# Grid attention with half-block column order: 256 keys for every query block, one bias transfer a head

## What is computed

```python
def neighbourhood_attn(q, k, v, rpb):
    rows = S // GRID_W                       # 8
    kr = min(NA_ROWS_MAX, rows)              # 8: every row
    row_start = jnp.clip(r - kr // 2, 0, rows - kr)
    col_start = jnp.clip(c - NA_COLS // 2, 0, GRID_W - NA_COLS)
    in_win = (c[None, :] >= col_start[:, None]) & (c[None, :] < col_start[:, None] + NA_COLS)
    bias = rpb.astype(jnp.float32)[:, dr_idx][:, :, :, dc_idx]
    s = jnp.einsum('brchd,brijhd->bhrcij', qg, kband).astype(jnp.float32) * (D ** -0.5)
    s = s + bias[None]
    s = jnp.where(in_win[None, None, None, :, None, :], s, NEG_INF)
    p = jax.nn.softmax(s.reshape(sh[:-2] + (kr * GRID_W,)), axis=-1).reshape(sh)
    o = jnp.einsum('bhrcij,brijhd->brchd', p.astype(v.dtype), vband)
```

## Time and profile before

| what | value |
|---|---|
| median of 3 runs | 2036.09 us (2034.68 to 2036.15) |
| the profiled execution | 2036.51 us, its span 2034.7 us |
| granted TensorE clock | 0.998 of full speed, mean |
| PE busy | 2008.6 us, 99% of the span |
| DVE, ACT, POOL busy | 54%, 43%, 9% |
| DMA | 175.00 MB, mean 86 GB/s |

### The profile page before, as it was taken

One profiled execution on the slowest core, in us unless ns is written; L12 is line 12 of the kernel. 1 busy time (PEld: TensorE's weight loads), 2 busy tenths in 40 slices (PEclk: granted clock), 3 DMA queues, 4 the chain that ended last, 5 costly groups with the idle time before them and its releaser, 6 DMA issues.

```text
span 2034.7 us, 31733 instructions
## 1 busy us (share of the span) xinstructions
PE 2008.6 (99%) x11679; PEld 1760.7 (87%) x11679; DVE 1091.6 (54%) x1898; ACT 868.4 (43%) x1272; POOL 189.5 (9%) x191
## 2 busy tenths in 40 slices
PE   8999999999999999999999999999999999999998
PEld 8989999999888888889988888888889888888887
DVE  4224788656653666567754433444656654434443
ACT  5534555533222544456743322233656543312233
POOL 0004001210110110001001100110014001100100
PEclk9999999999999999999999999999999999999999
DMA  4322111232333233331023332332322133332332
GB/s 137 98 82 83 53 43 51 64 94 86 94 109 106 87 93 98 113 99 52 12 85 94 100 103 83 93 108 86 100 83 66 34 100 93 104 92 86 100 98 79
DMA packets 321921, 175.00 MB, mean 86 GB/s; under 512 B 6560, under 2 KB 319136, under 8 KB 321840
## 3 DMA queue, kind: packets, MB, share of 16 engines
q1 hardware_dynamic: 321840, 173.92, 29.4%
HBM read 171.80 MB, written 2.10 MB: 85 GB/s over the span
## 4 chain that ended last, share of the span: by engine, by line
PE 67%; ACT 1%; DVE 1%; issue 1%; POOL 0%; POOLq 0%; ACTq 0%; DVEq 0%
PE ps L2086 38%; PE ps L2092 19%; PE ps L2680 3%; PE ps L2640 2%; PE ps L2665 2%; PE ps L2617 1%; PE ps L2618 1%; ACT scaled_heads L1224 1%; PE ps L2559 1%; DVE scaled_heads L1896 1%; PE ps L2718 0%; ACT w_hi L797 0%; PE ps L2204 0%; DVE w_lo L1303 0%; PE ps L2464 0%
## 5 line engine op out<-in xcount | busy, mean ns | idle before, releaser
L2086 PE MATMUL ps<-z_hi,w_hi 128*128 128x512 f32 (+2 forms) x2128 | 643.2, 343 | 0.8 <-DVE qf L1416 0.6
L2086 PE MATMUL ps<-z_lo,w_hi 128*128 128x512 f32 (+2 forms) x2128 | 634.4, 338 | 0.0
L1303 DVE TENSOR_TENSOR w_lo<-raw,w_hi 128x1024 fp32r<-128x1024 f32 (+2 forms) x298 | 384.9, 1292 | 434.6 <-ACT w_hi L797 433.3
L797 ACT ACTIVATE w_hi<-raw 128x1024 fp32r<-128x1024 f32 (+2 forms) x298 | 328.3, 1102 | 441.9 <-PE ps L2092 403.8
L2092 PE MATMUL ps<-z_hi,w_lo 128*128 128x512 f32 (+2 forms) x2128 | 446.1, 339 | 0.0
L2086 PEld LDWEIGHTS ps<-z_hi,w_hi 128*128 128x128 f32 x2128 | 366.4, 188 | 51.8 <-issue 4.2
L2086 PEld LDWEIGHTS ps<-z_lo,w_hi 128*128 128x128 f32 x2128 | 365.0, 188 | 44.8
L2092 PEld LDWEIGHTS ps<-z_hi,w_lo 128*128 128x128 f32 x2128 | 345.1, 188 | 45.3
L2086 PE MATMUL ps<-g_hi,w_hi 128*128 128x512 f32 (+1 forms) x539 | 209.4, 390 | 0.5 <-POOL g_lo L725 0.5
L2086 PE MATMUL ps<-g_lo,w_hi 128*128 128x512 f32 (+1 forms) x539 | 208.7, 389 | 0.0
L725 POOL TENSOR_TENSOR g_lo<-gv,g_hi 128x512 f32 x66 | 85.7, 1298 | 1064.5 <-ACT g_hi L1169 1064.5
(11 more groups left out here) (334 smaller groups left out, 2345.3 us busy)
## 6 DMA issues: line engine op xcount, KB each, us to landing
raw<-w_gate_up SPq DMA_DIRECT2D x88, 512.0 KB, 3.7
raw<-w_down SPq DMA_DIRECT2D x48, 704.0 KB, 4.4
raw<-w_in SPq DMA_DIRECT2D x44, 512.0 KB, 3.7
raw<-w_up SPq DMA_DIRECT2D x44, 512.0 KB, 3.7
raw<-w_out SPq DMA_DIRECT2D x24, 512.0 KB, 3.7
raw<-w_in_b SPq DMA_DIRECT2D x14, 512.0 KB, 3.7
raw<-w_in_a SPq DMA_DIRECT2D x12, 512.0 KB, 3.7
raw<-w_branch SPq DMA_DIRECT2D x8, 512.0 KB, 3.7
```

The costliest lines, as they stand in the source:

```text
L797: act.activation(w_hi[s][:, 0:width], raw[s][:, 0:width], ACT.Copy).then_inc(hi_done, 1)
L1303: dve.tensor_tensor(w_lo[s][:, 0:width], raw[s][:, 0:width], w_hi[s][:, 0:width].bitcast(F32), ALU.subtract).then_inc(lo_done, 1)
L2086: pe.matmul(out, w_hi[s][:, w0 + k * P:w0 + (k + 1) * P], rhs[:, lo:lo + width], start=a, stop=False)
```

## The change

Blocks of keys are now 128 tokens made of two half blocks of 8 columns, and all tokens of layer 1 except queries are turned by one half block: the last half block comes first. Key blocks b and b+1 (modulo 4) then hold columns from 8 before the query block to 8 behind it, so every query block has exactly 256 keys; block 3 takes key blocks 3 and 0 by a backward step. Queries, `q_pair`, are turned back by writing them in two pieces. Exponentials, masked sums, copies, transposes and value products of blocks 1 and 2 shrink with the width. The host lays out the biases as [12, 128, 256], so that one DMA brings a head's, and POOL adds the mask in three instructions of 256 columns. The diff, without what only follows from the new argument `l` of `span` and `key_block`, and without the constants' shapes:

```diff
+HB = BC // 2
         def natural(x):
-            return x.rearrange("p (r b c) -> p b r c", r=GRID_R, b=4)
+            return x.rearrange("p (r b c) -> p b r c", r=GRID_R, c=HB)
         def blocked(x):
-            return x.rearrange("p (b r c) -> p b r c", r=GRID_R, b=4)
+            return x.rearrange("p (b r c) -> p b r c", r=GRID_R, c=HB)
+        TURNED = ((slice(0, 7 * HD), slice(HD, SEQ)), (slice(7 * HD, SEQ), slice(0, HD)))
+        def turned_blocks(x):
+            return ((blocked(x)[:, 1:], slice(0, 7)), (blocked(x)[:, 0:1], slice(7, 8)))
-        def span(memory, b):
-            return (0, NMEM) if memory else ((P, 2 * P), (0, 3 * P), (0, 3 * P), (0, 2 * P))[b]
-        def key_block(memory, b, j):
-            return j if memory else max(b - 1, 0) + j
+        def span(memory, b, l):
+            return (0, NMEM) if memory or l else ((P, 2 * P), (0, 3 * P), (0, 3 * P), (0, 2 * P))[b]
+        def key_block(memory, b, j, l):
+            if memory:
+                return j
+            return (b + j) % 4 if l else max(b - 1, 0) + j
             def bias_load(h, r):
                 sp.wait_ge(*atts[1].at("bias", h - 2))
-                for rq in range(GRID_R):
-                    rows = slice(GRID_R - 1 - rq, 2 * GRID_R - 1 - rq)
-                    sp.dma_start(rpb_raw[r][rq * BC:(rq + 1) * BC, :, :],
-                                 t["rpb"][bass.ds(h, 1), :, rows, :].rearrange("o c r x -> (o c) r x"))\
-                      .then_inc(rpb_loaded[r], 16)
+                sp.dma_start(rpb_raw[r][:, :], t["rpb"][bass.ds(h, 1), :, :].rearrange("o q x -> (o q) x"))\
+                  .then_inc(rpb_loaded[r], 16)
-                        pool.wait_ge(rpb_loaded[r], 128 * g + 128)
+                        pool.wait_ge(rpb_loaded[r], 16 * g + 16)
                         pool.wait_ge(*s.at("ls", 4 * h - 8))
...
+                        for v in range(3):
+                            mask = att_con[:, 3 * P + 4 * HB * v:3 * P + 4 * HB * (v + 1)]
                             x = pool.tensor_tensor(
-                                bias[l][r][:, at_:at_ + n * P].rearrange("p (n r c) -> p n r c", n=n, r=GRID_R),
-                                rpb_raw[r][:, :, x0:x0 + n * BC].rearrange("p r (n c) -> p n r c", n=n),
-                                mask.rearrange("p (n o c) -> p n o c", n=n, o=1)
-                                    .to_broadcast([P, n, GRID_R, BC]), ALU.add)
+                                blocked(bias[l][r][:, v * NMEM:(v + 1) * NMEM]), blocked(rpb_raw[r][:, :]),
+                                mask.rearrange("p (n o c) -> p n o c", o=1, c=HB).to_broadcast([P, 4, GRID_R, HB]),
+                                ALU.add)
                         if order:
-                            z, x, square = (ur, vr)[s][:, 0:tokens], natural(x), blocked(square)
+                            z, x = (ur, vr)[s][:, 0:tokens], natural(x)
...
-                            act.activation(blocked(z), x, ACT.Identity, scale=g(m)).then_inc(sems["z"], 1)
+                            for to, blocks in turned_blocks(z):
+                                done = act.activation(to, x[:, blocks], ACT.Identity, scale=g(m))
+                            done.then_inc(sems["z"], 1)
                             act.wait_ge(*sems.at("z", m + 1))
                             act.activation(hi, z, ACT.Copy).then_inc(sems["z_hi"], 1)
+                            for to, blocks in turned_blocks(square):
+                                done = act.activation(to, x[:, blocks], ACT.Square)
+                            done.then_inc(sems["sq"], 1)
# rounded_heads, ACT:
-                    act.activation(hi, tile, ACT.Copy).then_inc(s["q_hi"], 1)
+                    if l and (m < queries or m >= queries + keys):
+                        for to, of in TURNED:
+                            done = act.activation(hi[:, :, to], tile[:, :, of], ACT.Copy)
+                    else:
+                        done = act.activation(hi, tile, ACT.Copy)
+                    done.then_inc(s["q_hi"], 1)
# rest_heads, DVE:
-                    dve.tensor_tensor(lo, tile, hi.bitcast(F32), ALU.subtract).then_inc(s["q_lo"], 1)
+                    if l and (m < first_key or m >= first_key + keys):
+                        for to, of in TURNED:
+                            done = dve.tensor_tensor(lo[:, :, to], tile[:, :, of], hi[:, :, to].bitcast(F32), ALU.subtract)
+                    else:
+                        done = dve.tensor_tensor(lo, tile, hi.bitcast(F32), ALU.subtract)
+                    done.then_inc(s["q_lo"], 1)
# scores, PE:
+                    if l and not memory and b == 3:
+                        bank = chunked(bank, 2)
+                        hi, rest_ = (chunked(x[:, head, :], 4)[:, ::-3] for x in (hi, rest_))
+                    else:
+                        hi, rest_ = (x[:, head, lo:lo + width] for x in (hi, rest_))
# laid_out, host:
-    padded = np.pad(a["rpb_b_2"][0], ((0, 0), (0, 0), (BC, BC + 1)))
-    out["rpb"] = np.stack([padded[:, :, BC - 1 - c:4 * BC - 1 - c] for c in range(BC)], axis=1)
+    q, key = np.arange(P)[:, None], np.arange(NMEM)[None, :]
+    down = key // HB % GRID_R - q // HB % GRID_R + GRID_R - 1
+    across = key // HD * HB - HB + key % HB - (q // HD * HB + q % HB) + BC - 1
+    out["rpb"] = a["rpb_b_2"][0][:, down, np.clip(across, 0, 2 * BC - 2)]
```

More of the change, by code:

```diff
@@ L202, in build @@
         ls_second = [sb([tails[b]], f"ls1_{b}", [P, 3 * P]) for b in range(4)]
[L203 removed]
+        rpb_raw = [sb([w_at[i] + 4 * UNIT], f"rpb_raw{i}", [P, NMEM]) for i in range(2)] + [rpb_last]
         assert at[0] <= scratch
@@ L1244, in exps @@
                     for b in blocks:
-                        lo, width = span(memory, b)
+                        lo, width = span(memory, b, l)
                         act.activation(ls(r, b)[:, lo:lo + width], ls(r, b)[:, lo:lo + width], ACT.Exp,
@@ L1250, in copy @@
                 def copy(h, memory, b):
-                    _, width = span(memory, b)
+                    _, width = span(memory, b, l)
                     act.wait_ge(*s.at("t", 4 * h + (b + 1)))
@@ L2611, in scores @@
                     memory = n_ >= QH
-                    _, width = span(memory, b)
+                    _, width = span(memory, b, l)
                     bank = banks(r + b)[:, 0:width]
-                    lo = key_block(memory, b, 0) * P
+                    lo = key_block(memory, b, 0, l) * P
                     hi, rest_ = (mk_hi, mk_lo) if memory else (k_hi, k_lo)
                     head = n_ - QH if memory else kv
-                    pe.matmul(bank, q_pair[:, n_, b * P:(b + 1) * P], hi[:, head, lo:lo + width], start=True, stop=False)
-                    pe.matmul(bank, q_pair[:, n_, b * P:(b + 1) * P], rest_[:, head, lo:lo + width],
-                              start=False, stop=True).then_inc(s["s"], 1)
+                    if l and not memory and b == 3:
+                        bank = chunked(bank, 2)
+                        hi, rest_ = (chunked(x[:, head, :], 4)[:, ::-3] for x in (hi, rest_))
+                    else:
+                        hi, rest_ = (x[:, head, lo:lo + width] for x in (hi, rest_))
+                    pe.matmul(bank, q_pair[:, n_, b * P:(b + 1) * P], hi, start=True, stop=False)
+                    pe.matmul(bank, q_pair[:, n_, b * P:(b + 1) * P], rest_, start=False, stop=True).then_inc(s["s"], 1)
                 for half in range((1, 2)[l]):
@@ L2658, in turn @@
                 def turn(h, r, memory, b):
-                    _, width = span(memory, b)
-                    lo = span(memory, b)[0]
+                    _, width = span(memory, b, l)
+                    lo = span(memory, b, l)[0]
                     pe.wait_ge(*s.at("exp", 4 * h + (b + 1)))
@@ L2674, in values @@
                     for j in range(width // P):
-                        block = key_block(memory, b, j)
+                        block = key_block(memory, b, j, l)
                         if memory:
```

38 lines of the change are left out of this document (16 added, 22 removed).

## The result

| | kernel before | changed kernel |
|---|---|---|
| executions timed side by side | 5 | 5 |
| median | 2036.09 us | 2024.18 us |
| lowest to highest | 2034.64 to 2036.17 | 2024.04 to 2025.51 |
| the profiled execution (span) | 2036.51 (2034.7) | 2025.51 (2023.7) |

The ratio is 0.9946, with a 95% interval of 0.9932 to 0.996: half a per cent faster, a small gain but clear of the noise.

What follows compares the result with a forecast made beforehand. PE, busy 99% of 2034.7 us, was taken as the bound. Terms -10.7 + 0.2 + 1.2 + 0.1 = -9.2 us, taken from 2036.51 and 2036.09, gave 2027.3 and 2026.9; forecast 2027.1, range 2025.2 to 2030.6.

Steps and rivals of the forecast that it cites:

- The matmuls, -10.7: Layer 1's twelve grid heads: narrower scores, transposes and value products take 0.89 us a head off PE, 10.7 us in all.
- (a): Step 2 of layer 1's head loop: time saved on block 1 only lengthens PE's wait for ACT's copy, +0.2 us.
- The backward read: Block 3's keys in layer 1, read backwards in two pieces: 0 to 2.4 us more over 24 matmuls, nearest to 0.
- (b): Layer 1's grid steps: DVE's negation of row maxima, delayed by POOL, makes PE wait about 0.2 us a step, +1.2 us.
- the meeting: Layer 1's head loop: POOL starts on the negation's event as in layer 0, lengthening the negation from 0.16 to 0.8 us.
- the room: Delay the grid negation can have before PE waits for block 1's values: some 0.44 us, against a delay of 0.63.
- Rival one: Layer 1's head loop: negation not delayed or room enough, PE stays the bound; 10.4 us off, 2025.8 us; chance 0.22.
- Rival three: Layer 1's head loop: negation waits for three POOL adds, 9 to 12 us lost, 2034.7 to 2038 us; chance 0.03.
- (c): Turned queries in two pieces: extra ACT and DVE instructions shift PE's wait before the second value unit, +0.1 us.
- (d): Turned norm in layer 0's last FFN quarter: 16 more ACT instructions of about 0.2 us, covered, 0.
- (e): Bias transfers: one DMA a head in place of eight, PE waits for no weight there, gain 0.

Runs made afterwards that it cites:

- e4: Changed kernel with block 3 reading key blocks 2 and 3 forwards in one piece, not 3 and 0 backwards; 2024.31 to 2027.94 us, ratio 0.9951.
- e11: Changed kernel with POOL's first two adds of a grid bias released one score block earlier; 2024.66 to 2026.37 us, ratio 0.9949.
- e3: Changed kernel without the turning, queries and norm written in one piece in natural block order; 2024.33 to 2027.86 us, ratio 0.9957.
- e6: Changed kernel with POOL's adds of biases 0 and 1 held back in layer 1 for five more weight splits; 2023.47 to 2025.6 us, ratio 0.9951.
- e7: Kernel before with one bias transfer a head in place of eight; 2034.87 to 2036.25 us in nine executions, 2037.69 in one, ratio 1.0004.
- e2: Changed kernel with eight bias transfers a head in place of one, new layout kept; 2029.0 to 2030.59 us, ratio 0.9972.
- e9: Changed kernel with POOL's biases of grid heads 4 to 11 held until the negation two heads before is done; 2024.16 to 2025.88 us, ratio 0.9949.

## Why the prediction was right and where it was wrong

**The matmuls, -10.7: right.** The head loop and the scores in the value stage gave 10.03 + 0.42 = 10.45 us, which is 10.7 less the 0.2 that step (a) gives back. In step 2 PE waits 0.34 us for ACT's copy, until 1541.02: the values start 0.63 us behind the scores in front of them (1540.39), against 0.45 before (1541.53 to 1541.98). The backward read, for which there was no row, was taken at 0, its near bound, and e4 confirms it.

**(b) The negation, +1.2: this step failed.** It put a PE wait of about 0.2 us into each of seven steps, behind ACT's copy of block 1. None of the three traces of the changed kernel has such a wait behind step 2, whose one wait belongs to (a). Three things in the step were wrong.

First the meeting: "POOL starts on the same event as the negation, as in layer 0" is true, but the negation is 0.11 us ahead in layer 1 and takes 0.16, where 0.8 was forecast. In layer 0, where POOL's add starts 0.04 to 0.05 us after it, it takes 0.89. I carried the row of layer 0 over to a case in which POOL starts 0.06 us later, and took the start order for settled. In layer 1 the rule cited from the Trainium skill (SBUF — State Buffer, section Who interferes with whom) held: the negation, first by 0.11 us, was not held up. Layer 0's rows differ from it if the start that the profile shows is the issue.

Second a reading: before, POOL "mostly misses the negation" is not what the trace has. Eight of the twelve grid negations of the kernel before take 0.27 to 0.91 us, in a loop whose steps had no PE gap. Two of them:

```profile
1545.43 0.57 DVE L1982 SCALAR_TENSOR_TENSOR neg_max<-row_max 128x4 f32<-128x4 f32 x1
...
1566.97 0.63 DVE L1982 SCALAR_TENSOR_TENSOR neg_max<-row_max 128x4 f32<-128x4 f32 x1
```

Third the room: 0.44 us was computed, 0.53 to 0.55 is what e11 and e4 give. The largest part of the difference is the time from the end of ACT's copy to PE's start, taken as 0.15 from step 2; in e4 it is 0.05 (1549.22 + 0.36 to 1549.63). The negations in the train are 0.47 us late and fit into that room; one of 0.8 us, 0.64 late, would have cost some 0.1 us a step, half of what was computed.

Rival one, "negation not delayed, or room enough", was right: the first behind the train, the second in it. With 0 for 1.2 the sum is 10.4 us off, against 10.6 by the traces.

**Rival three, 0.03: present, but as a rare event.** I spoke against it with one row, a negation of 0.91 us beside nine adds, and priced it in each of five to seven steps, for a train of three. In the one trace that has it, it strikes a single negation in the backlog, for 3.65 us with the clock's fall behind it. A single trace that shows an instruction lucky once is no evidence that it always is.

**(c) +0.1: the sign is wrong, the size negligible.** The wait at the second value unit went from 1.01 to 0.89, not up; e3 shows that the turned pieces are 0.15 of the 0.89, and e6 that POOL's adds are 0.60, which I named but did not separate. (d) is right, 0 within what e3 can tell: its lowest time is 0.3 us above the changed kernel's, not below.

**(e) One transfer a head, 0: right against the kernel before (e7), incomplete as a reading.** It is no extra gain, but the condition under which the 10.7 can be had: without it 4.9 us of them are lost (e2). Its "the data is there long before" was used to price the negation and not to ask what the eight transfers would cost at the new pace.

**The median.** The rest is the base. I set 2036.51 and 2036.09 as the point to start from, and the three times of before (2034.68 to 2036.15) already showed a distance that has nothing to do with the change: the clock's fall near 868 us, 1.3 to 1.5 us. The differences to the forecast are 1.2 for the negation, 0.2 for (c), 0.2 because the forecast starts from about 2036.3 and the median is 2036.09, and 1.3 because before's median is of the upper level and after's of the lower: 2.9, as measured. That the two medians fell on different levels is chance. With (b) and (c) right and both medians on one level the time would have been 2025.5, inside the range. So the step between the levels took the median out of the range, and (b) is the largest error of the sum itself. The range should have gone down by one level, to about 2023.9.

## What to carry to other kernels

When a loop is cut to a shorter step, redo every "hidden" price at the new pace: the transfers were free at 4.3 us a step and worth 4.9 us at 3.4. A small instruction that is seen to end only with the long, back-to-back instructions of another engine should not meet them on the critical path; order them with a wait on the small one, which cost nothing here (e9), since POOL's adds had slack. And read how the shown times of a kernel are spread before choosing the base of a forecast: two levels in three runs are worth as much as a term of the sum.

## What the runs showed of the hardware

- A 128x4 instruction of VectorE that was held up beside POOL's adds ended, in the traces shown, within 0.1 us of the end of an add: the one under way (0.35 to 0.64 us), the next (1.30) or the last of the train (2.69). It did so with two SBUF inputs and with one.
- Behind a gap of 1.83 us on PE the granted clock fell: the stretches shown under e4 read 0.79, 0.50 (1.2 GHz) and 0.86, which cost about as much again as the gap. Behind a gap of 0.45 us (e11) the windows up to 1554 read 1.00.
- The fall near 868 us comes without such a gap: in the traces of before and after PE has 5.95 us busy of the 6.00 in front of it (860 to 866), and 2.00 of 2.00 in each window of it. It is in 6 of the 14 traces, whose kernels do not differ in this stretch; why it comes in one execution and not in another is not known.
- POOL's add of 128x256 with a pattern of runs of 8 and a broadcast mask takes 0.69 us from start to start, flat 0.57. VectorE's split of 128x768 takes 0.94 us alone and 1.48 beside such adds.
